# Two-layer-block kernel on one core: order of the vector engine's work in the first feed-forward layer, and the way the norms are summed and spread

## The reference, cut to what matters

```python
def rmsnorm(x, g):
    y = x * lax.rsqrt(jnp.mean(x * x, axis=-1, keepdims=True) + EPS)
    return y * g

hf = rmsnorm(x, norm_ff_g[l])                          # the norm n2
z = jax.nn.relu(jnp.einsum('bsd,df->bsf', hf, w_ff1))  # 1024 -> 4096
x = x + jnp.einsum('bsf,fd->bsd', z * z, w_ff2)        # 4096 -> 1024
return rmsnorm(x, norm_final_g)
```

## Time and profile before

| what | value |
|---|---|
| median of 3 runs | 1570.07 us (1569.48 to 1571.84) |
| the profiled execution | 1571.68 us |
| its span | 1569.9 us |
| mean granted TensorE clock | 0.973 of full |
| PE busy | 1510.3 us, 96% of the span |
| DVE busy | 804.0 us, 51% |
| ACT busy | 562.6 us, 36% |

### The profile page before, as it was taken

How to read it: one execution, slowest core, us unless ns; L and a number is a source line. 1 busy time by engine, 2 the same in 40 slices (tenths; PEclk the granted TensorE clock), 3 DMA queues, 4 the chain that set the end, 5 groups by cost and what they waited for, 6 DMA issues and landing times.

```text
span 1569.9 us, 18627 instructions
## 1 busy us (share of the span) xinstructions
PE 1510.3 (96%) x6586; PEld 1198.4 (76%) x6586; DVE 804.0 (51%) x1108; ACT 562.6 (36%) x759; POOL 28.6 (2%) x68
## 2 busy tenths in 40 slices
PE   6999999999999999999997998999898999999997
PEld 5887888888887788888886764555686888888885
DVE  7344221652455656656677535445357552663564
ACT  4343222323233313232244333433435541551342
POOL 1000000000000000000000000000000000000000
PEclk7999999999999999999998999999898999999998
DMA  5333323233222553545344120110022233323221
GB/s 169 106 101 101 105 82 107 81 107 105 82 85 78 186 186 121 187 160 187 120 162 146 54 81 27 38 43 28 27 82 79 91 103 101 100 87 107 80 81 53
DMA packets 135788, 158.15 MB, mean 101 GB/s; under 512 B 2513, under 2 KB 129071, under 8 KB 135743
## 3 DMA queue, kind: packets, MB, share of 16 engines
q1 hardware_dynamic: 129024, 131.08, 25.9%
q0 software_dynamic: 6240, 26.30, 5.0%
q10 hardware_dynamic: 479, 0.17, 0.0%
HBM read 155.44 MB, written 2.10 MB: 100 GB/s over the span
## 4 chain that ended last, share of the span: by engine, by line
PE 89%; DVE 4%; ACT 3%; issue 2%; DMA 1%; DVEq 0%; SPq 0%; ACTq 0%
PE bank L395 27%; PE bank L397 27%; PE bank L396 27%; PE aux L637 1%; PE aux L632 1%; PE aux L653 1%; ACT weights_hi L693 1%; DMA gates<-in_x 1%; PE aux L435 1%; DVE ada_sums L1226 1%; PE aux L641 1%; DVE weights_lo L1001 1%; PE aux L416 1%; PE aux L509 1%; PE aux L581 0%
## 5 line engine op out<-in xcount | busy, mean ns | idle before, releaser
L395 PE MATMUL bank<-operand_hi,weights_hi 128*128 128x512 f32 x1936 | 768.0, 397 | 10.9 <-DVE operand_lo L1013 4.9
L396 PE MATMUL bank<-operand_lo,weights_hi 128*128 128x512 f32 x1936 | 757.8, 391 | 0.0
L397 PE MATMUL bank<-operand_hi,weights_lo 128*128 128x512 f32 x1936 | 757.6, 391 | 0.0
L395 PEld LDWEIGHTS bank<-operand_hi,weights_hi 128*128 128x128 f32 x1936 | 366.2, 189 | 109.6 <-issue 31.0
L397 PEld LDWEIGHTS bank<-operand_hi,weights_lo 128*128 128x128 f32 x1936 | 366.0, 189 | 77.1
L396 PEld LDWEIGHTS bank<-operand_lo,weights_hi 128*128 128x128 f32 x1936 | 366.6, 189 | 74.8 <-issue 1.0
L1001 DVE TENSOR_TENSOR weights_lo<-raw,weights_hi 128x1024 fp32r<-128x1024 f32 (+1 forms) x244 | 295.9, 1213 | 189.4 <-ACT weights_hi L693 182.8
L693 ACT ACTIVATE weights_hi<-raw 128x1024 fp32r<-128x1024 f32 (+1 forms) x244 | 253.1, 1043 | 182.0 <-PE bank L397 176.0
L1011 DVE TENSOR_TENSOR operand_lo<-value,operand_hi 128x512 f32 (+1 forms) x90 | 62.2, 692 | 94.8 <-ACT operand_hi L698 94.8
L698 ACT ACTIVATE operand_hi<-value 128x512 f32 (+1 forms) x90 | 56.9, 632 | 124.0 <-DVE value L1163 34.0
L1388 DVE SCALAR_TENSOR_TENSOR conv_or_gate<-bank,vector_table,conv_or_gate 128x511 f32<-128x511 f32 x44 | 32.9, 747 | 79.9 <-ACT conv_or_gate L959 78.1
(11 more groups left out here) (178 smaller groups left out, 749.6 us busy)
## 6 DMA issues: line engine op xcount, KB each, us to landing
raw<-in_w_in SPq DMA_DIRECT2D x40, 1024.0 KB, 5.1
raw<-in_w_ff SPq DMA_DIRECT2D x32, 1024.0 KB, 5.8
ada_or_attention<-in_w_ada POOLq DMA_DIRECT2D x16, 1536.0 KB, 7.5
raw<-in_w_up SPq DMA_DIRECT2D x22, 1024.0 KB, 5.1
raw<-in_w_out SPq DMA_DIRECT2D x8, 1024.0 KB, 5.0
raw<-in_w_down SPq DMA_DIRECT2D x8, 1024.0 KB, 5.0
raw<-in_w_proj_a SPq DMA_DIRECT2D x4, 1024.0 KB, 4.9
raw<-in_w_proj_b SPq DMA_DIRECT2D x4, 1024.0 KB, 5.0
```

The source lines that it names most:

```text
L395: pe.matmul(ps[k][:, :], wh, ah, start=(kt == 0), stop=False)
L396: pe.matmul(ps[k][:, :], wh, al, start=False, stop=False)
L397: mm = pe.matmul(ps[k][:, :], wl, ah, start=False, stop=(kt == k_tiles - 1))
```

## The change

Four things change.

1. **DVE's order in part 0 of each ff chunk.** `weights(q + 1, k)` now stands ahead of `rest(...)`. ACT's program stays as it was.
2. **The first ff quad.** `sum_squares("n2")` moves behind kt = 2 of tiles 0 and 1, `spread_rms("n2")` behind kt = 5, and both stand inside these two tiles; the ada turn and tiles 2 and 3 follow.
3. **The last addition of squares** goes away for n1, n2, n3, n4 and final (not "between"): DVE adds seven, and PE runs 4 tiny matmuls on the sum and 4 more, accumulating, on the last square itself. Two DVE loops are written out for this, with the ff loop's last chunk.
4. **The diagonals** (L1031) go away for all six norms: PE multiplies a broadcast column of the reciprocals by the identity, in four 128x128x128 matmuls in place of one with 512 columns.

```diff
             def sum_squares(norm):
+                if norm == "between":
+                    pe.wait_ge(sum_added, summed(norm, 9))
+                    for b in range(NBLK):
+                        mm = pe.matmul(aux[0][:, b:b + 1], ssum[:, b * P:(b + 1) * P], mean_w, start=True, stop=True)
+                    mm.then_inc(norm_summed, 1)
+                    return
                 if norm == "n3":
-                    pe.wait_ge(sum3_added, 9)
-                    sums = ssum3
+                    pe.wait_ge(sum3_added, 8)
+                    sums, last = ssum3, sq3[1]
                 else:
-                    pe.wait_ge(sum_added, 9 * SUM[norm] + 9)
-                    sums = ssum[:, :]
+                    pe.wait_ge(sum_added, summed(norm, 8))
+                    sums, last = ssum[:, :], tb(1)
                 for b in range(NBLK):
-                    mm = pe.matmul(aux[0][:, b:b + 1], sums[:, b * P:(b + 1) * P], mean_w, start=True, stop=True)
+                    pe.matmul(aux[0][:, b:b + 1], sums[:, b * P:(b + 1) * P], mean_w, start=(b == 0), stop=False,
+                              skip_group_check=True)
+                if norm == "n3":
+                    pe.wait_ge(sq3_done, 8)
+                else:
+                    pe.wait_ge(sq_done, 8 * SUM[norm] + 8)
+                for b in range(NBLK):
+                    mm = pe.matmul(aux[0][:, b:b + 1], last[:, b * P:(b + 1) * P], mean_w, start=False,
+                                   stop=(b == NBLK - 1), skip_group_check=True)
                 mm.then_inc(norm_summed, 1)

             def spread_rms(norm, bank=1):
-                pe.wait_ge(diag_done, NORM[norm] + 1)
-                pe.matmul(aux[bank][:, :], ones[:, :], spread[:, :], start=True, stop=True).then_inc(norm_spread, 1)
+                pe.wait_ge(inv_done, NORM[norm] + 1)
+                for b in range(NBLK):
+                    mm = pe.matmul(aux[bank][:, b * P:(b + 1) * P],
+                                   rms[:, NBLK + b:NBLK + b + 1].to_broadcast([P, P]), ident[:, :], start=True, stop=True)
+                mm.then_inc(norm_spread, 1)
...
             def first_ff_quad():
                 q = F["ff"]
-                stream(q, (0, 1), 1, made(MADE["n2"]))
+                stream(q, (0, 1), 1, made(MADE["n2"]), first=0, last=3)
                 sum_squares("n2")
+                stream(q, (0, 1), 1, made(MADE["n2"]), first=3, last=6)
+                spread_rms("n2")
+                stream(q, (0, 1), 1, made(MADE["n2"]), first=6)
                 ada_turn(0)
-                stream(q, (2,), 1, first=0, last=4)
-                spread_rms("n2")
-                stream(q, (2,), 1, first=4)
-                stream(q, (3,), 1)
+                for k in (2, 3):
+                    stream(q, (k,), 1)
...
             def invert_rms(name):
                 dve.wait_ge(rms_done, NORM[name] + 1)
                 dve.reciprocal(rms[:, NBLK:2 * NBLK], rms[:, 0:NBLK]).then_inc(inv_done, 1)
-                dve.wait_ge(inv_done, NORM[name] + 1)
-                dve.tensor_tensor(spread[:, :].rearrange("p (b n) -> p b n", b=NBLK),
-                                  ident[:, :].unsqueeze(1).to_broadcast([P, NBLK, P]),
-                                  rms[:, NBLK:2 * NBLK].unsqueeze(2).to_broadcast([P, NBLK, P]),
-                                  ALU.mult).then_inc(diag_done, 1)
                 dve.wait_ge(norm_spread, NORM[name] + 1)
...
+            def all_but_last_square(name):
+                def work(n, q, k):
+                    if n < KT - 1:
+                        add_square(name, n, k % 2)
+                return work
...
                         if part == 0:
                             dve.scalar_tensor_tensor(out=tb(k % 2), in0=ps[k][:, :], scalar=0.0, in1=spread[:, :],
                                                      op0=ALU.max, op1=ALU.mult).then_inc(bank_read[k], 1)
+                            weights(q + 1, k)
                             rest(0, n, tA[k % 2][:, :], MADE["ff"] + KT * c + n)
                         else:
                             grow_x(n, q, k)
-                        if not last or part == 0:
-                            weights(q + 1, k)
+                            if not last:
+                                weights(q + 1, k)
```

More of the change, by code:

```diff
@@ L257, in build, with summed @@
         SUM = {name: n for n, name in enumerate(["n1", "n2", "between", "n4", "final"])}
+        def summed(name, n):
+            whole = [m for m in SUM if SUM[m] < SUM[name]]
+            return sum(9 if m == "between" else 8 for m in whole) + n
         def rows(w):
@@ L1124, in _, with quad @@
             dve.memset(acc[:, :], 0.0).then_inc(ada_step, 1)
+            def quad(name, i, work, after):
+                for k in range(4):
+                    q = F[name] + i
+                    if work is not None:
+                        dve.wait_ge(tile_done, 4 * q + k + 1)
+                        work(4 * i + k, q, k)
+                    if after is not None:
+                        after(4 * i + k, q, k)
+                    weights(q + 1, k)
             def phase(name, work, after=None, n=2):
                 with dve.Fori(0, n) as i:
[L1129 to L1135, removed]
-                        weights(q + 1, k)
+                    quad(name, i, work, after)
+            def all_but_last_square(name):
[3 more added lines that the diff above has]
+                return work
             def product(dst, src):
@@ L1183, in split_x, with split_and_sum @@
                                          op1=ALU.subtract).then_inc(operand, 1)
-            def split_and_add_square(n, q, k):
+            def split_and_sum(n, q, k):
                 dve.wait_ge(bank_read[k], q + 1)
                 split_x(n)
-                add_square("n2", n, k % 2)
-            phase("out", grow_x, split_and_add_square)
+                all_but_last_square("n2")(n, q, k)
+            for i in range(2):
+                quad("out", i, grow_x, split_and_sum)
             invert_rms("n2")
@@ L1192, in _, with ff_quad @@
             dve.wait_ge(n2_rms_kept, 1)
[L1194 to L1197, removed]
+            def ff_quad(c, part, i, last):
+                for k in range(4):
+                    q = F["ff"] + 4 * c + 2 * part + i
+                    n = 4 * i + k
+                    piece = 4 * c + 2 * part + i
+                    dve.wait_ge(tile_done, 4 * q + k + 1)
+                    if part == 0:
+                        dve.wait_ge(value, VALUED["ff"] + KT * c + n - 1)
+                        dve.scalar_tensor_tensor(out=tb(k % 2), in0=ps[k][:, :], scalar=0.0, in1=spread[:, :],
+                                                 op0=ALU.max, op1=ALU.mult).then_inc(bank_read[k], 1)
+                        weights(q + 1, k)
+                        rest(0, n, tA[k % 2][:, :], MADE["ff"] + KT * c + n)
+                    else:
+                        grow_x(n, q, k)
+                        if not last:
+                            weights(q + 1, k)
+                    if k == 1:
+                        dve.wait_ge(ada_landed, 16 * (piece + 1))
+                        dve.wait_ge(ada_turned, piece + 1)
+                    if k in (1, 2):
+                        for kt in range(4 * (k - 1), 4 * k):
+                            src = ada_raw[:, kt * ADA:(kt + 1) * ADA]
+                            if kt == 0:
+                                dve.tensor_scalar(acc[:, :], src, cvec[:, kt:kt + 1], None, ALU.mult)\
+                                   .then_inc(ada_step, 1)
+                            else:
+                                dve.wait_ge(ada_step, 1 + KT * piece + kt)
+                                dve.scalar_tensor_tensor(out=acc[:, :], in0=src, scalar=cvec[:, kt:kt + 1],
+                                                         in1=acc[:, :], op0=ALU.mult, op1=ALU.add)\
+                                   .then_inc(ada_step, 1)
+                    if last and part == 1:
+                        add_square("between", n, k % 2)
+                        if n < KT - 1:
+                            dve.wait_ge(sq3_done, n + 1)
+                            dve.wait_ge(sum3_added, n + 1)
+                            dve.tensor_tensor(ssum3, ssum3, sq3[k % 2], ALU.add).then_inc(sum3_added, 1)
+                        weights(q + 1, k)
@@ L1198, in ff_chunk @@
+            def ff_chunk(c):
                 for part in range(2):
                     with dve.Fori(0, 2) as i:
[L1200 to L1212, removed]
[L1213 to L1234 removed]
@@ L1236, in _, with last_ff_chunk @@
+                        ff_quad(c, part, i, False)
+            def last_ff_chunk(c):
+                clear_sum()
+                dve.memset(ssum3, 0.0).then_inc(sum3_added, 1)
+                for part in range(2):
+                    for i in range(2):
+                        ff_quad(c, part, i, True)
             dve.wait_ge(c_ready, 1)
             with dve.Fori(0, 3) as c:
```

(4 more changed lines are left out.)

32 lines of the change are left out of this document (8 added, 24 removed).

## The result

The changed kernel takes 1605.82 us (median of 4 runs, 1603.38 to 1606.69) against 1570.95 beside it: 34.9 us more, ratio 1.0215 with a 95% interval of 1.0192 to 1.0238. I had forecast slower, by 27.3 us. The direction and the place were right, the size fell 1.8 us outside my range (1586 to 1604).

What follows compares the result with a forecast made beforehand. PE was taken to set the pace (22.45 us a quad), DVE's chain near it (22.05). Stalls 19.5, chunk 0 3.4, norms -3.6 and clock 8 sum to 27.3 us, giving 1597.4 us, range 1586 to 1604.

Steps and rivals of the forecast that it cites:

- What bounds the kernel: Feed-forward part 0: PE sets the pace at 22.45 us a quad, DVE's dependent chain close behind at 22.05.
- The mechanism: Part 0: low weights still wait for ACT's high weights, the residue follows them; PE stalls about 6.5 us before kt = 7.
- The rival in which the residue slips into its old gap: Part 0: DVE pulls the residue ahead of the waiting low weights, making the order's whole term zero; other side's chance 0.06.
- The addition of a tile: Part 0 on DVE: the residue behind the low weights lengthens each tile by 0.80 us, between 0.69 and 0.83.
- The wait at the start of part 1: Start of part 1: tile 1's low weights late by some 0.3 us, swallowed by the later wait at kt = 7.
- The clock: Behind the four new stalls, PE's clock falls to 1.2 GHz, costing 2.0 us each: +8 us, bounds 0 and 11.
- the long low clock: Rival, chance 0.08: after each stall the clock stays low longer, 4 x 2.8 = 11, a tile's addition 0.83; 1602 us.
- n2 and the norms: First ff quad: DVE starts 4.2 us earlier, tiny matmuls cost PE 0.79; n1, n3, n4 and final together -3.6 us.
- The rival in which the residue costs nothing: Part 0, chance 0.06: behind the weights the residue adds no time, chunk 0's stalls go too; -6.4, 1563.7 us.
- The transfers: Feed-forward loads are unaffected: raw weights are asked for a quad ahead, ada pieces move by the same few us.

Runs made afterwards that it cites:

- both weights first: Changed kernel, DVE's new order kept, with ACT also making the high weights first in part 0; 1564.91 us, ratio 0.9938.
- the order alone: Kernel before with only DVE's residue and low-weights instructions exchanged in part 0; 1610.43 us, ratio 1.0237.
- both orders: Kernel before with high weights first on ACT and low weights first on DVE in part 0, nothing else; 1566.97 us, ratio 0.9956.
- The filled stall: Changed kernel plus 24 useless matmuls per chunk in front of kt = 7 in part 1's first quad; 1594.44 us, ratio 1.0122.
- the diagonals back: Changed kernel with DVE's old order, and the diagonals with one wide matmul restored; 1569.41 us, ratio 0.997.
- the last tile only: Changed kernel with DVE's new order kept only for k = 3 of each part 0 quad, old order for the others; 1577.47 us, ratio 1.0027.
- n2 back: Changed kernel with DVE's old order, and n2's sums and spread in their old places; 1571.13 us, ratio 0.9987.
- the last addition back: Changed kernel with DVE's old order, and the eighth addition of squares back on DVE for all norms; 1568.68 us, ratio 0.9983.

## Why the prediction was right or wrong, point by point

**What bounds the kernel: right.** PE's period of 22.45 us a quad against DVE's chain of 22.05 was the whole case. The first was kept, the second became 26.1 (I had said 25), and PE stood still where part 1 needs the last residue. The version with both weights first shows that the chain can be 17.5 us (22.45 less 4.95).

**The mechanism: right.** The low weights didn't start earlier (3.17 for 3.16 us), because ACT's order wasn't changed; the residue lost its gap. Undoing the order takes the loss away, the order alone brings it, and making ACT deliver earlier takes it away too. That the exchange gains anything beyond this shows only on the kernel before, where chunk 0 still had waits (4.2 us shorter with both orders). The rival in which the residue slips into its old gap is refuted by the rows: it started 2.1 us after its input was complete.

**The addition of a tile: undersized, 0.96 for 0.80 us.** From chunk 1's first evacuation to that of tile 7 it takes 46.42 us for 40.11; with the 0.40 of idle time that went, seven additions are 6.71 us. I had bounded it by the residue's 0.69 and 0.83, its distance to the next instruction. But 0.83 was its distance to the low weights; now something else stands behind it: 0.96 us to the next evacuation, 0.91 to the ada step, 0.81 where ada steps go on, and 1.43 at the end of the loop's body (620.50 to 621.93).

**The wait at the start of part 1: missed.** I had it at 0.3 us and swallowed by the later one; it is 1.38 us, and is indeed swallowed. With it the delay of chunk 1 adds up: kt = 7 was due 43.5 us behind the ada turn (596.12), at 639.6, and began at 647.30, 7.7 us late, for a forecast of 6.5. The longer additions are 1.1 us of the difference. In chunk 3, where the low weights were in time, the wait at kt = 7 was 5.5 us.

**The clock: undersized, 4.0 for 2.0 us a stall.** This is the step that failed most. The filled stall gives 15.8 us for the four, where I had 8 with a bound of 11. I priced it by the stretches behind the norms (10 matmuls in 4.0 us), on the ground that the stalls are as long. But there only the end of a low stretch fell on full-sized work. At n3 of the kernel before the clock was low already at the sums, 7.8 us before the matmuls of the earlier trace rows: the four tiny matmuls of the sums took 1.86 us, at full clock 0.95:

```profile
853.24 1.86 PE L429 MATMUL aux<-mean_columns,conv_or_gate 128*128 128x1 f32 x8 [4.44 <-DVE conv_or_gate L1233]
```

Behind the new stalls the whole low stretch, 7.4 to 9.5 us, fell on such work. The length of the stall doesn't give the price either: with the order alone stalls of the same 5.8 us cost 1.4 us more than their length (chunks of 99.0 us against 97.6 with the stall filled) where they cost up to 4.4 in the changed kernel. Why the clock came back sooner there, no run shows.

**What put the result outside the range.** The spans differ by 34.7 us for the 27.3 of the sum. The clock took 7.8 us more than forecast, standing still in the feed-forward layer 3.0 more, and the stretches from n3 on 3.6 less. Had either of the first two been of its forecast size, the result would have been inside. The nearest rival was that of the long low clock, 1602 us, right in kind, but it too had only 2.8 us a stall.

**n2 and the norms: right** (-4.8 for -4.9 us at the first mark in the trace; in final the 0.57 us behind the table load are gone; the run that has the diagonals back is 3.1 us slower, for 3.0). The rival in which the residue costs nothing gave 1563.7 us; the run without the order's part came out at 1566.3.

**n3 to n4: not foreseen.** This stretch took 4.3 us less, 0.8 of which are n4's. The window over most of it:

```profile
910.00:1215.00 305.00, 291.02 (x1195) 194.32 (x1194) 138.74 (x254) 116.47 (x195) 9.35 (x32) 0.98 0.16 49
```

PE's mean granted clock there is 0.98, in a window at the same place of the kernel before (870 to 1180 us) 0.96. Only n4's part of the change is in this stretch. It took between 324.2 and 331.3 us over all versions, and the three with long or repeated stalls in the layer before it have the smallest values (324.2, 324.3 and 325.5, the others from 326.5). Whether that is chance in single profiles or comes of the stalls is open. It hid a part of the loss: the feed-forward layer alone lost 45.1 us (4.8 of them the earlier start), of which I had forecast 34.4.

**The transfers** played no part, as said: no wait of PE or ACT for a load came up in the layer.

## What to carry to other kernels

Before two instructions of an engine are exchanged, look for what each waits for: the one brought forward gains only if its input is there earlier, and the one put behind inherits its wait. Here the input came from another engine, and the exchange cost nothing only when that engine's order was changed with it. An engine at 61% can be the bound: compare the period of its dependent chain, not its busy share, with the period of the engine that it feeds. A stall on TensorE is to be priced at its length and the low clock behind it, which here cost from nothing to 4.4 us each time, and from 1.4 to 4.4 behind stalls of one length.

## What the runs showed of the hardware

- Stalls of PE of 5.5 to 5.8 us were followed by 7.4 to 9.5 us at 1.2 GHz in the changed kernel, and cost 3.4 to 4.4 us more than their length; in the kernel with the order alone the low clock lasted 3.8 to 4.0 us and cost 1.4 (chunks of 99.0 us against 97.6 with the clock held). The Trainium skill, page TensorE: Matmul & The Clock Gate, section HAM oscillation — how this bites in real kernels, describes the same pattern, idle time in each period that makes the next one start cold; the trace agrees, in each of the four chunks.
- With the last tile only, three stalls of 2.2 us were followed by low clock (3.5 us lost each), and one of 1.6 us was not; nor were those of 2.0 us in the kernel before (the clock from 493 to 545 us is 1.00) and of 2.1 us with n2 back. With the last addition back, a wait of 2.1 us and eight tiny matmuls behind it were followed by low clock from 488.9 to 492.3 us, so the length of the wait doesn't decide alone.
- An instruction of DVE that waits for the result of the one before starts 0.81 to 0.96 us after the start of a predecessor of 0.69 us, and 1.43 across the turn of a loop, where an independent one follows at 0.60 us (842.40 and 843.00 in the kernel before).
- A broadcast column as the stationary operand costs nothing measurable: in the chain of the changed kernel the four matmuls of 128 columns took 0.89 us at full clock and 2.09 at half, in that of the kernel before the one of 512 columns 0.87 and 2.09.
